# Forward substitution of the delta rule's diagonal blocks: from VectorE to GpSimd

## The chip, the cores and the metric

The kernel runs on one core of one Trainium2 chip. Its engines work side by side, each from an instruction queue of its own: TensorE (PE in the profile, PEld for its weight loads), VectorE (DVE), ScalarE (ACT), GpSimd (POOL) and the sync engine (SP), which here issues most of the transfers. They wait for one another by semaphores. The metric is device time in microseconds (us); less is better.

## The reference, cut to what matters

Two transformer blocks run one behind the other over 256 tokens of width 1024, all in float32. The first block has three mixers: a softmax attention with decay ("fox"), a stick-breaking attention, and a gated delta rule in chunks. The change lies in the delta rule, and what stands around it in the queues is the stick-breaking attention.

```python
def gated_delta_rule(q, k, v, g, beta):
    ...
    kk = jnp.einsum("nbhcd,nbhed->nbhce", kc, kc)
    a_mat = jnp.where(strict, bc[..., :, None] * kk * decay, 0.0) + jnp.eye(CHUNK, dtype=f32)
    ...
    sol = lax.linalg.triangular_solve(a_mat, rhs, left_side=True, lower=True)

def stick_breaking_attention(q, k, v):
    ...
        log_keep = jnp.where(mask, -jax.nn.softplus(z), 0.0)
        ...
        a = jnp.exp(jnp.where(mask, z + rc, -jnp.inf)).astype(vh.dtype)
```

The kernel inverts the unit lower triangular matrix of each head and each of two tiles of 128 tokens: first its 16x16 diagonal blocks by forward substitution, then it joins blocks of 16 to 32, 64 and 128 by products on TensorE.

## The kernel before

**Weights.** All weight matrices are cut into blocks of 128x2048 float32, numbered in order of use: gdn 0 to 5, sbqk 6 to 9, sbv 10 and 11, foxqk 12 to 15, foxv 16 and 17, gate_c 18 to 21, out_c 22 and on. A block is loaded in two halves by the sync queue into RAW, which has room for two blocks. So that TensorE can multiply in fp32r, ScalarE makes HI, the rounded block (L1480), and VectorE LO, the rest RAW - HI (L2019). Each has room for four blocks. `split_ahead(phase, Turn(j))` makes HI or LO of the block that stands four behind block j of the phase; on ScalarE it waits until TensorE is through with block j. The load of block n into RAW waits for LO of block n - 2, half by half. TensorE makes three products for each weight tile (L826, L827, L828): HI with XH, HI with XL, LO with XH.

**The substitution.** VectorE writes the delta rule's matrix into DL (delta_L, L2171) from the keys' products `kk0` and `kk1`. The sync queue takes its 64 diagonal blocks of 16x16 to HBM in eight transfers (L621) and back as DIAG_L (L623), one block to a partition: 64 partitions, 16x16 numbers. VectorE waits for diag_loaded and solves in 15 steps of two instructions each (L2189, L2190), every one linked to the one before by a semaphore; step j works on (j+1) x (15-j) numbers in each partition, which makes 680 over the 15 steps. The last sets diag_solved.

**What is queued around it.** On VectorE: LO of block 15; the absolute value of Z for the stick-breaking attention (L2180); the substitution; `split_ahead("foxqk", Turn(0))`, that is LO of block 16; the keep chain L2196 to L2198, which makes SP_ and needs ScalarE's Ln (keep_ln); LO of 17; LO of 18; then stick_arg, the subtraction of TensorE's sums from Z, for heads 0 and 1; LO of 19; stick_arg for heads 2 and 3; the heads' norm (heads_norm 1, which needs ScalarE's squares, then a root on GpSimd, then L2079) and LO of 20.

On the sync queue, after DIAG_L: a wait for diag_solved; the store of DIAG_T to HBM (L625); the load of block 18; a wait for the store; eight transfers into the diagonal of MP (L635); the loads of block 19 and on.

On ScalarE: HI of 16; Exp and Ln of SP_ (L1620, L1621); half of foxqk's result; HI of 17; HI of 18; the other half of foxqk's result; HI of 19; two squares for the heads' norm (L1630); HI of 20; the Exp of Z (L1635, stick_ready); foxv's result; HI of 21; a wait for diag_stored.

On TensorE: the blocks of foxqk 0 to 2; a wait for keep_ready; the sums rest_sums (L1078 to L1081) for heads 0 and 1; foxqk 3; those for heads 2 and 3; foxv; a wait for stick_ready; the products with the values (L1099, L1100); gate_c 0 (block 18); a wait for diag_placed and the turns T16 of MP (L983); gate_c 1 (block 19); the turns of the fox heads out of X (L983), then gate_c 2 (block 20).

On GpSimd: long before, the masks and the zeroing of MP and DIAG_T; two LO blocks (ON_POOL_CONV); `heads_root(0)`; a wait for the keys' products being taken; `heads_root(1)` (L710, L703, L704); then the products of DL with the level masks into MA (L789).

Of the kernel before, what the change touches and what calls it, by code (L numbers as in the profile page):

```python
# [193 lines left out]
N_DIAG = NT * HEADS * (P // 16)  # L194


def build(nc, A, out):
    f32, f32r = mybir.dt.float32, mybir.dt.float32r
    ALU = mybir.AluOpType
# [22 lines left out]
    with ctx:  # L222
# [37 lines left out]
        def at(name, kib, shape, dt=f32):  # L260
            size = 4
            for s in shape[1:]:
                size *= s
            assert kib * 1024 + size <= ARENA, name
            return nc.alloc_sbuf_tensor_at(name, shape, dt, offset=base + int(kib * 1024))
# [10 lines left out]
        DIAG_L, DIAG_T, DIAG_TERM = (at(f"diag_{n}", 40 + i, [N_DIAG, 16, 16]) for i, n in enumerate(["L", "T", "term"]))  # L276
# [87 lines left out]
        def sems(names):  # L364
            return [sem(n) for n in names.split()]
# [30 lines left out]
        diag_zeroed, diag_written, diag_loaded, diag_solved, diag_stored, diag_placed = sems(  # L396
            "diag_zeroed diag_written diag_loaded diag_solved diag_stored diag_placed")
# [38 lines left out]
        def small(name):  # L436
            return SMP[:, SMALL_ORDER[name] % 4, :]
# [11 lines left out]
        def small_is_taken(eng, name):  # L449
            eng.wait_ge(small_taken[SMALL_ORDER[name] % 4], SMALL_ORDER[name] // 4 + 1)  # L450
# [39 lines left out]
        def col(name, i=0):  # L490
            tile, row = COL_AT[name]
            return COL[tile][:, row + i:row + i + 1]
# [33 lines left out]
        def every(mask, n):  # L526

            return mask.unsqueeze(1).broadcast_to([P, n, mask.shape[1]])

        def by_head(ap, d=P):  # L530
            return ap.rearrange("p (h d) -> p h d", d=d)
# [140 lines left out]
        def _(pool):  # L672
            steps = [0]

            def link(ins):
                steps[0] += 1
                ins.then_inc(pool_step, 1)
                pool.wait_ge(pool_step, steps[0])
# [21 lines left out]
            def inverse_root(name, mean_square):  # L700

                n = ROOTS[name]
                link(pool.tensor_scalar(mean_square, mean_square, EPS, None, ALU.add))  # L703
                pool.tensor_tensor(ROOT[name], mean_square, MINUS_HALF[:, 0:n], ALU.pow).then_inc(root_ready, 1)  # L704

            def heads_root(n, mult):

                pool.wait_ge(heads_sums, NT * (n + 1))
                if mult != 1.0:
                    link(pool.tensor_scalar(HSS[n], HSS[n], mult, None, ALU.mult))  # L710
                inverse_root(f"heads{n}", HSS[n])
# [67 lines left out]

            for t in range(NT):  # L780
                small_is_taken(pool, f"kk{t}")
            heads_root(1, 1.0 / DH)


# [1222 lines left out]
        def _(dve):  # L2007
            steps = [0]

            def link(ins):  # L2010

                steps[0] += 1
                ins.then_inc(dve_step, 1)
                dve.wait_ge(dve_step, steps[0])
# [11 lines left out]
            def split_ahead(phase, t, halves=range(2)):  # L2026

                n = FIRST[phase] + t.j + RING
                if n < N_BLOCKS and n not in ON_POOL:
                    for half in halves:  # L2030
                        lo_half(n, half, t.count(lambda j: 2 * (FIRST[phase] + j + RING) + half + 1))
# [78 lines left out]
            for j in range(6):  # L2110
                dve.wait_ge(conv_base, 2 * j + 2)
                for i in range(2):
                    tile = 2 * j + i
                    u = acc("gdn", Turn(j))[:, i * 256:(i + 1) * 256]
                    for back in (1, 2, 3):
                        y = CONVF[:, tile, back:SEQ]
                        ins = dve.scalar_tensor_tensor(out=y, in0=u[:, 0:SEQ - back], scalar=col("gdn_conv", (3 - back) * 12 + tile),
                                                       in1=y, op0=ALU.mult, op1=ALU.add)
# [49 lines left out]
            for t in range(NT):  # L2168
                small_is_done(dve, f"kk{t}")
                for h in range(HEADS):  # L2170
                    ins = dve.scalar_tensor_tensor(out=DL[:, t, h, :], in0=small(f"kk{t}")[:, h * P:(h + 1) * P],  # L2171
                                                   scalar=BETA[:, t, h:h + 1], in1=MA[:, t, h, :], op0=ALU.mult, op1=ALU.mult)
# [6 lines left out]
                small_is_taken(dve, f"z{h}")  # L2179
            dve.scalar_tensor_tensor(out=SP_[:, :, :], in0=Z[:, :, :], scalar=-1.0, in1=Z[:, :, :], op0=ALU.mult, op1=ALU.max).then_inc(keep_abs, 1)  # L2180

            dve.wait_ge(diag_loaded, 16)
            dve.wait_ge(diag_zeroed, 3)
            for j in range(15):
                n, m = j + 1, 15 - j
                below = DIAG_L[:, n:16, j:n].rearrange("b r o -> b o r").broadcast_to([N_DIAG, n, m])
                solved = DIAG_T[:, 0:n, j:n].broadcast_to([N_DIAG, n, m])
                rest = DIAG_T[:, 0:n, n:16]
                link(dve.tensor_tensor(DIAG_TERM[:, 0:n, 0:m], below, solved, ALU.mult))  # L2189
                ins = dve.tensor_tensor(rest, rest, DIAG_TERM[:, 0:n, 0:m], ALU.subtract)  # L2190
                if j < 14:
                    link(ins)
            ins.then_inc(diag_solved, 1)
            split_ahead("foxqk", Turn(0))
            dve.wait_ge(keep_ln, 1)
            link(dve.scalar_tensor_tensor(out=SP_[:, :, :], in0=Z[:, :, :], scalar=0.0, in1=SP_[:, :, :], op0=ALU.max, op1=ALU.add))  # L2196
# [371 lines left out]
            for g in range(4):  # L2568
# [4 lines left out]
                for i in range(2):  # L2573
                    d = 2 * g + i
                    ins = dve.scalar_tensor_tensor(out=by_head(G[:, d, :]), in0=by_head(small(name)[:, i * SEQ:(i + 1) * SEQ]),
                                                   scalar=col("sgu_norm_g_2", d), in1=every(BS[:, g, :], NT),
                                                   op0=ALU.mult, op1=ALU.add)
# [42 lines left out]
            for c in range(2):  # L2620
                cols = slice(c * 512, (c + 1) * 512)
                a, b = Turn(2 * c), Turn(2 * c + 1)
# [82 lines left out]
```

## Time and profile before

| | us |
|---|---|
| median of 3 runs | 1179.21 (1178.56 to 1179.53) |
| profiled execution, its own time | 1175.5 |
| its span, first to last instruction | 1173.5 |
| TensorE busy | 1145.9 (98%) |
| VectorE busy | 744.9 (63%) |
| ScalarE busy | 589.5 (50%) |
| GpSimd busy | 97.6 (8%) |

The durations in the rows below come from the one profiled execution, whose mean granted TensorE clock was 0.997 of full speed. In a timeline row stand the start, the duration, the engine, the line, the operation, output and inputs, and in brackets how long the engine was idle before and what it waited for.

### The profile page before, as it was taken

How to read it: one execution, taken by the hardware profiler on the slowest of the kernel's cores; microseconds unless marked ns; L12 is line 12 of the kernel's file. 1: busy time of each engine (PE TensorE's matmuls, PEld its weight loads, DVE VectorE, ACT ScalarE, POOL GpSimd, SP SyncE). 2: the span in 40 equal slices, each digit the busy share in tenths (PEclk: the TensorE clock that was granted, in tenths of full speed). 3: DMA queues.
4: the chain of work that ended last, by engine and by line, in shares of the span. 5: the costliest groups of instructions: out<-in, count | busy, mean ns of one | idle time of the engine just before them, and what ended most of it. 6: DMA issues, size and time to landing. Idle time of an engine off the chain costs nothing.

```text
span 1173.5 us, 16543 instructions
## 1 busy us (share of the span) xinstructions
PE 1145.9 (98%) x6464; PEld 1003.2 (85%) x6464; DVE 744.9 (63%) x922; ACT 589.5 (50%) x781; POOL 97.6 (8%) x156
## 2 busy tenths in 40 slices
PE   7999999998999999999999999999989999999997
PEld 7998888897887999988888898799878878889885
DVE  5767767657666788764565454565775576554455
ACT  5675544444455666543454444454464355444352
POOL 5310211001010000000000000200500010000021
PEclk9999999999999999999999999999999999999999
DMA  8734564455553675556475556475465567555642
GB/s 237 219 119 140 162 201 139 129 176 186 177 187 119 216 224 175 191 193 202 135 242 184 177 177 215 143 227 158 138 222 193 176 191 249 180 178 179 207 135 71
DMA packets 124060, 210.33 MB, mean 179 GB/s; under 512 B 10980, under 2 KB 60249, under 8 KB 123993
## 3 DMA queue, kind: packets, MB, share of 16 engines
q1 hardware_dynamic: 120393, 199.17, 53.4%
q10 hardware_dynamic: 3504, 10.22, 2.5%
q8 instruction: 47, 0.77, 0.3%
q0 software_dynamic: 96, 0.01, 0.1%
q14 instruction: 20, 0.16, 0.0%
HBM read 208.19 MB, written 1.18 MB: 178 GB/s over the span
## 4 chain that ended last, share of the span: by engine, by line
PE 87%; DVE 6%; ACT 3%; issue 1%; DMA 1%; POOL 1%; SPq 0%; POOLq 0%; DVEq 0%; ACTq 0%
PE ACCP L826 26%; PE ACCP L828 26%; PE ACCP L827 26%; PE SMP L983 3%; DVE LO L2019 3%; PE SMP L976 2%; ACT HI L1480 1%; PE SMP L826 1%; PE SMP L828 1%; PE SMP L827 1%; DMA PRE_GAIN<-in_norm_mix_dram 1%; POOL STAT L704 0%; DMA diag_L<-scratch_diag_l 0%; POOL STAT L703 0%; DVE U L2582 0%
## 5 line engine op out<-in xcount | busy, mean ns | idle before, releaser
L2019 DVE TENSOR_TENSOR LO<-RAW,HI 128x1024 fp32r<-128x1024 f32 x367 | 439.1, 1235 | 242.5 <-ACT HI L1480 235.1
L1480 ACT ACTIVATE HI<-RAW 128x1024 fp32r<-128x1024 f32 x366 | 369.6, 1054 | 275.2 <-PE ACCP L828 240.9
L826 PE MATMUL ACCP<-HI,XH 128*128 128x512 f32 x688 | 271.1, 394 | 2.1 <-ACT SV L1488 1.6
L828 PE MATMUL ACCP<-HI,XL 128*128 128x512 f32 x688 | 268.1, 390 | 0.0
L827 PE MATMUL ACCP<-LO,XH 128*128 128x512 f32 x688 | 267.8, 389 | 0.0
L826 PE MATMUL ACCP<-XH,HI 128*128 128x256 f32 x688 | 196.6, 286 | 1.9 <-DVE XL L2064 1.9
L827 PE MATMUL ACCP<-XL,HI 128*128 128x256 f32 x688 | 195.4, 284 | 0.0
L828 PE MATMUL ACCP<-XH,LO 128*128 128x256 f32 x688 | 195.4, 284 | 0.0
L826 PEld LDWEIGHTS ACCP<-HI,XH 128*128 128x128 f32 x688 | 129.2, 188 | 28.5 <-issue 1.7
L828 PEld LDWEIGHTS ACCP<-HI,XL 128*128 128x128 f32 x688 | 129.1, 188 | 27.3
L827 PEld LDWEIGHTS ACCP<-LO,XH 128*128 128x128 f32 x688 | 129.3, 188 | 25.8
L826 PEld LDWEIGHTS ACCP<-XH,HI 128*128 128x128 f32 x688 | 132.9, 193 | 2.4 <-DVE LO L2019 2.2
L827 PEld LDWEIGHTS ACCP<-XL,HI 128*128 128x128 f32 x688 | 132.9, 193 | 0.1
L828 PEld LDWEIGHTS ACCP<-XH,LO 128*128 128x128 f32 x688 | 132.8, 193 | 0.0
L826 PE MATMUL ACCP<-HI,HH 128*128 128x512 f32 x328 | 128.1, 390 | 0.0
L828 PE MATMUL ACCP<-HI,HL 128*128 128x512 f32 x328 | 127.7, 389 | 0.0
L827 PE MATMUL ACCP<-LO,HH 128*128 128x512 f32 x328 | 127.6, 389 | 0.0
L703 POOL TENSOR_SCALAR STAT<-STAT 128x1 f32<-128x1 f32 (+3 forms) x30 | 11.6, 385 | 804.3 <-ACT XS L1736 453.1
L828 PEld LDWEIGHTS ACCP<-HI,HL 128*128 128x128 f32 x328 | 61.6, 188 | 12.7
L827 PEld LDWEIGHTS ACCP<-LO,HH 128*128 128x128 f32 x328 | 61.6, 188 | 12.6
L826 PEld LDWEIGHTS ACCP<-HI,HH 128*128 128x128 f32 x328 | 61.6, 188 | 12.6
L1488 ACT ACTIVATE XH<-SMP 128x512 fp32r<-128x512 f32 x36 | 20.5, 596 | 39.8 <-PE SMP L983 39.5
(379 smaller groups left out, 1146.4 us busy)
## 6 DMA issues: line engine op xcount, KB each, us to landing
RAW<-in_w_in_dram SPq DMA_DIRECT2D x104, 512.0 KB, 4.5
RAW<-in_w_up_dram SPq DMA_DIRECT2D x44, 512.0 KB, 4.6
RAW<-in_ffn_w_gate_dram SPq DMA_DIRECT2D x44, 512.0 KB, 4.5
RAW<-in_ffn_w_up_dram SPq DMA_DIRECT2D x44, 512.0 KB, 4.4
RAW<-in_ffn_w_down_dram SPq DMA_DIRECT2D x44, 512.0 KB, 4.3
RAW<-in_w_down_dram SPq DMA_DIRECT2D x22, 512.0 KB, 4.2
RAW<-in_w_out_dram SPq DMA_DIRECT2D x8, 512.0 KB, 4.0
RAW<-in_w_mkv_dram SPq DMA_DIRECT2D x8, 512.0 KB, 3.8
```

What stands on the lines that cost most here:

```text
L703: link(pool.tensor_scalar(mean_square, mean_square, EPS, None, ALU.add))
L826: pe.matmul(dst, lhs[0], rhs[0], start=start, stop=False)
L827: pe.matmul(dst, lhs[0], rhs[1], start=False, stop=False)
L828: return pe.matmul(dst, lhs[1], rhs[0], start=False, stop=stop)
L976: last = pe.matmul(small(name)[:, h * P:(h + 1) * P], lhs, rhs, start=True, stop=True)
L983: last = pe.transpose(small(name)[:, h * P:(h + 1) * P], source(h), IDENT[:, :])
L1480: act.activation(HI[:, n % RING, half_of(half)], RAW[:, n % RAWS, half, :], ACT.Copy).then_inc(hi_ready, 1)
L1488: act.activation(dst, src, ACT.Copy, scale=scale).then_inc(signal, 1)
L2019: dve.tensor_tensor(LO[:, s, c], RAW[:, n % RAWS, half, :], HI[:, s, c].bitcast(f32), ALU.subtract).then_inc(lo_ready[s], 1)
```

## The change

The 30 instructions of the substitution move from VectorE's program to GpSimd's, with their two waits (diag_loaded, diag_zeroed) and with the signal diag_solved. On GpSimd they stand between the wait for the keys' products and `heads_root(1)`. On VectorE `split_ahead("foxqk", Turn(0))` follows L2180 directly. Both engines have a helper `link` that does the same with a semaphore of their own. Operands, shapes and all transfers stay as they are.

```diff
             for t in range(NT):
                 small_is_taken(pool, f"kk{t}")
+            pool.wait_ge(diag_loaded, 16)
+            pool.wait_ge(diag_zeroed, 3)
+            for j in range(15):
+                n, m = j + 1, 15 - j
+                below = DIAG_L[:, n:16, j:n].rearrange("b r o -> b o r").broadcast_to([N_DIAG, n, m])
+                solved = DIAG_T[:, 0:n, j:n].broadcast_to([N_DIAG, n, m])
+                rest = DIAG_T[:, 0:n, n:16]
+                link(pool.tensor_tensor(DIAG_TERM[:, 0:n, 0:m], below, solved, ALU.mult))
+                ins = pool.tensor_tensor(rest, rest, DIAG_TERM[:, 0:n, 0:m], ALU.subtract)
+                if j < 14:
+                    link(ins)
+            ins.then_inc(diag_solved, 1)
             heads_root(1, 1.0 / DH)
...
             dve.scalar_tensor_tensor(out=SP_[:, :, :], in0=Z[:, :, :], scalar=-1.0, in1=Z[:, :, :], op0=ALU.mult, op1=ALU.max).then_inc(keep_abs, 1)
 
-            dve.wait_ge(diag_loaded, 16)
-            dve.wait_ge(diag_zeroed, 3)
-            for j in range(15):
-                n, m = j + 1, 15 - j
-                below = DIAG_L[:, n:16, j:n].rearrange("b r o -> b o r").broadcast_to([N_DIAG, n, m])
-                solved = DIAG_T[:, 0:n, j:n].broadcast_to([N_DIAG, n, m])
-                rest = DIAG_T[:, 0:n, n:16]
-                link(dve.tensor_tensor(DIAG_TERM[:, 0:n, 0:m], below, solved, ALU.mult))
-                ins = dve.tensor_tensor(rest, rest, DIAG_TERM[:, 0:n, 0:m], ALU.subtract)
-                if j < 14:
-                    link(ins)
-            ins.then_inc(diag_solved, 1)
             split_ahead("foxqk", Turn(0))
```

## Rows read from the trace of the kernel before

**Rows 1.** Page, part 1: busy us, share of the span, instructions.

```profile
PE 1145.9 (98%) x6464; PEld 1003.2 (85%) x6464; DVE 744.9 (63%) x922; ACT 589.5 (50%) x781; POOL 97.6 (8%) x156
```

**Rows 2.** TensorE's waits (us, times, longest), and busy us between 120.7 and 172.

```profile
PE SMP L1078 <- DVE SP__72 L2198: 0.7, 1, 0.7
...
core 0: us, PE busy (x) PEld busy (x) DVE busy (x) ACT busy (x) POOL busy (x), PEclk, DMA share, GB/s
120.70:172.00 51.30, 51.30 (x269) 44.08 (x269) 35.47 (x34) 26.66 (x33) 10.49 (x7) 1.00 0.59 187
```

**Rows 3.** Timeline of VectorE around and behind the substitution.

```profile
107.88 0.17 DVE L2189 TENSOR_TENSOR diag_term<-diag_L,diag_T 64x15 f32<-64x15 f32 x1 [3.23 <-DMA diag_L<-scratch_diag_l]
...
115.15 2.34 DVE L2019 TENSOR_TENSOR LO<-RAW,HI 128x1024 fp32r<-128x1024 f32 x2
117.42 1.74 DVE L2196 SCALAR_TENSOR_TENSOR SP__72<-Z,SP__72 128x1536 f32<-128x1536 f32 x1
...
119.92 0.69 DVE L2198 TENSOR_TENSOR SP__72<-SP__72,BEFORE 128x512 f32<-128x512 f32 x1
...
140.04 4.53 DVE L2079 TENSOR_TENSOR X<-X,STAT 128x1024 f32<-128x1024 f32 x2 [3.87 <-POOL STAT L704]
```

**Rows 4.** Timeline of ScalarE from HI of 16 to the Exp of Z.

```profile
109.14 2.01 ACT L1480 ACTIVATE HI<-RAW 128x1024 fp32r<-128x1024 f32 x2 [5.42 <-PE ACCP L828]
...
113.84 1.49 ACT L1621 ACTIVATE SP__72<-SP__72 128x1536 f32<-128x1536 f32 x1
...
120.22 1.06 ACT L1480 ACTIVATE HI<-RAW 128x1024 fp32r<-128x1024 f32 x1 [2.02 <-DMA RAW<-in_w_in_dram]
122.13 1.06 ACT L1480 ACTIVATE HI<-RAW 128x1024 fp32r<-128x1024 f32 x1 [0.85 <-DMA RAW<-in_w_in_dram]
...
131.43 2.00 ACT L1630 ACTIVATE XS<-X 128x1024 f32<-128x1024 f32 x2
136.11 2.01 ACT L1480 ACTIVATE HI<-RAW 128x1024 fp32r<-128x1024 f32 x2 [2.68 <-PE ACCP L828]
...
139.43 1.49 ACT L1635 ACTIVATE Z<-Z 128x1536 f32<-128x1536 f32 x1
```

**Rows 5.** Timeline of the sync queue; last row: KB and us to landing.

```profile
115.25 0.47 SPq L625 DMA_DIRECT2D scratch_diag_t<-diag_T  x1
116.38 0.37 SPq L551 DMA_DIRECT2D RAW<-in_w_in_dram  x1
...
117.52 0.37 SPq L551 DMA_DIRECT2D RAW<-in_w_in_dram  x1
117.99 3.72 SPq L635 DMA_DIRECT2D delta_P<-scratch_diag_t  x8
...
scratch_diag_t<-diag_T SPq DMA_DIRECT2D x1, 64.0 KB, 1.9
```

**Rows 6.** Timeline of TensorE, three starts.

```profile
120.66 0.44 PE L1078 MATMUL SMP<-BIG_NOT_BEFORE_R,IDENT_R 128*128 128x384 f32 x1 [0.68 <-DVE SP__72 L2198]
...
141.35 0.59 PE L1099 MATMUL SMP<-Z,SV 128*128 128x256 f32 x2
...
155.77 1.91 PE L983 MATMUL SMP<-IDENT,X 128*128 128x128 f32 x16
```

**Rows 7.** Timeline of GpSimd: large and small instructions elsewhere in the kernel.

```profile
829.60 1.04 POOL L807 TENSOR_TENSOR S2A<-C 128x510 f32<-128x510 f32 x1
...
836.13 2.73 POOL L807 TENSOR_TENSOR S<-S2B 128x1524 f32<-128x1524 f32 x1
...
1164.57 0.58 POOL L816 TENSOR_TENSOR STAT<-STAT 128x1 f32<-128x1 f32 x1 [19.74 <-DVE STAT L2661]
1165.23 0.22 POOL L703 TENSOR_SCALAR STAT<-STAT 128x1 f32<-128x1 f32 x1
```

**Rows 8.** GpSimd and VectorE side by side: timelines, and VectorE's mean from 164.2 to 168.8.

```profile
950.04 1.12 POOL L703 TENSOR_SCALAR STAT<-STAT 128x1 f32<-128x1 f32 x1 [6.22 <-ACT XS L1736]
...
949.86 1.22 DVE L2019 TENSOR_TENSOR LO<-RAW,HI 128x1024 fp32r<-128x1024 f32 x1
...
L2019 DVE TENSOR_TENSOR LO<-RAW,HI 128x1024 fp32r<-128x1024 f32 x2 | 4.4, 2260 | 1.4 <-ACT HI L1480 1.4
...
164.13 3.52 POOL L789 TENSOR_TENSOR delta_A<-delta_L,LEVEL 128x512 f32<-128x512 f32 x2 [20.65 <-PE SMP L976]
```

## The prediction

> **What bounds the kernel now.** The page of the profile is read first: TensorE is busy 1145.9 of 1173.5 us and GpSimd 97.6 [rows 1]. So a microsecond leaves the time only where TensorE itself stands still. The waits by engine come next: of TensorE's few waits one lies beside the change, the 0.7 us in front of L1078 for VectorE's L2198 [rows 2]. The table by stretches shows the engine without a gap from 120.70 to 172.00 [rows 2]. The timelines of the five queues between 100 and 142 us then tell what everyone does around the substitution.
>
> VectorE waits 3.23 us for DIAG_L, starts the substitution at 107.88 and is through at 115.15. Then come LO of block 16 (split_ahead("foxqk", 0)) and the keep chain L2196 to L2198 [rows 3]; LO of blocks 17 and 18 follows. The chain ends at 120.61, TensorE starts L1078 at 120.66 [rows 3, 6].
>
> The sync queue hangs on the same event. Behind its wait on diag_solved stand, in this order: the store of DIAG_T (115.25), both halves of block 18 (116.38, 117.52), the eight transfers into MP from 117.99, and block 19 and all later weights [rows 5]. ScalarE works in order too: HI of 18, HI of 19, two squares up to 133.43, HI of 20 at 136.11, a table load, the Exp of Z from 139.43 to 140.92 [rows 4]. TensorE takes that Exp at 141.35 (L1099) [rows 6]. HI of 20 starts as TensorE finishes a foxv block. ScalarE has about 2.7 us of idle time in front of it, from 133.43 to 136.11, and 0.4 us behind the Exp. That is all the slack between the weights and TensorE here.
>
> **What leaves VectorE.** 30 instructions in 115.15 - 107.88 = 7.3 us, and the 3.2 us of waiting. LO of 16 can then follow HI of 16, ready in halves at about 110.2 and 111.15, and ends near 112.6. The keep chain waits for the Ln, which ends at 113.84 + 1.49 = 115.33 [rows 4]; its three instructions span 120.61 - 117.42 = 3.2 us [rows 3], so it ends at 118.5. TensorE reaches L1078 at 120.66 - 0.68 = 119.98, so the wait goes and 0.7 us is won, with 1.4 us to spare for disturbance by GpSimd. Nothing else on TensorE waits for VectorE up to 142: 0.7 us is the whole direct gain. LO of 17 follows up to about 121.
>
> **What GpSimd gets.** It is idle here in the trace of before: its next work is the root for which VectorE waits 3.87 us up to 140.04 [rows 3], so its queue itself delays nobody unless the end comes after 136. It starts when DIAG_L lands, 107.9. No row shows a small two-input product in short rows on it. From below: the adds of 510 and 1524 elements took 1.04 and 2.73 us [rows 7]. That is 1.69 / 1014 = 1.67 ns an element and 1.04 - 510 x 0.00167 = 0.19 us fixed. The mean instruction here has (sum of (j+1)(15-j) over 15 steps)/15 = 680/15 = 45 elements, 0.08 us; every step is linked, and a linked pair shows 0.08 us between its end at 1165.15 and the next start at 1165.23 [rows 7]. Sum 0.35 us, 30 of them 10.4 us. From above: an add of one element took 0.58 us [rows 7]; 0.58 + 0.08 + 0.08 = 0.74, times 30 = 22 us. I take 0.45, nearer to the lower end, since the large adds bear a small fixed part and the one-element add ran beside a VectorE instruction; with 0.1 us more for rows of 1 to 15 elements read at a stride of 64 bytes (estimate): 13.5 us.
>
> The Trainium skill (GPSIMD Engine Reference, Performance pitfalls for Q7 kernels) says that reads with a step over 8 bytes take about half again as long per element. No row of before shows it; on the 15 products alone it would add 680 x 0.83 ns = 0.6 us, an estimate from that page and the row's slope, and it is no term of the sum.
>
> **What the two engines do to each other.** A one-element GpSimd instruction that began at 950.04, just behind the start of a VectorE LO at 949.86 (ending 951.08), took 1.12 us and ended at 951.16; the same form took 0.22 elsewhere [rows 8, 7]. And two LO on VectorE beside GpSimd's masks took 2.26 us each [rows 8], where two in a row take 2.34 together [rows 3]. So they serialise where both read two operands. The Trainium skill (SBUF, Who interferes with whom) says that the later one blocks fully; the first pair agrees. By that rule alone, without any turn for GpSimd between VectorE's instructions, the sum below would be about 2 us later.
>
> Then, at 0.45 us each: 5 GpSimd instructions before LO of 16 starts (107.95 to 110.2); about one behind each of its two halves, 2; 6 between 112.6 and 115.4; one behind each of the three chain and two LO instructions, 5. That is 18 by 121.5. VectorE has then nothing to do, as block 18 is not there; the remaining 12 take 5.4 us. End E = 127, against 115.2 before.
>
> **What is late next.** From the end E, with durations of before. The store issues at once and lands 1.9 us later [rows 5]; block 18 issues at E + 0.5 and E + 0.95; the MP transfers start at E + 2.0 and take 3.72 (+0.06) us of the queue [rows 5]; block 19 issues at E + 5.8 and E + 6.25. A half's HI started 120.22 - 116.38 = 3.84 us behind its issue, the second 4.6 [rows 4, 5]. So HI of 18 ends at E + 6.6, LO of 18 at E + 7.9; block 20 issues at E + 6.75 and E + 7.95. HI of 19 ends at E + 6.25 + 4.6 + 1.06 = E + 11.9. Squares 2.0 and HI of 20, 2.0: E + 15.9 (its weights are there by E + 12.6). Table load 1.28, Exp 1.49 [rows 4]: E + 18.7. TensorE starts L1099 there, against 141.35. The change is E + 18.7 - 141.35 = E - 122.6, never under -0.7. At E = 127: +4.4 us. The 0.7 us is in it already.
>
> The other moved pieces cost nothing. MP is placed by E + 9.2 (the last of eight transfers issues at E + 5.3, and even the 3.84 us of a weight half would do), TensorE takes it behind L1099; ScalarE's wait on diag_stored stands behind the Exp as well. The squares end at E + 13.9 = 140.9 and not at 133.4, so the root on GpSimd, VectorE's scaled heads (L2079, ending at 144.6 before) and LO of 20 come 7.5 us later, 3 more than TensorE; TensorE turns those heads at 155.77 [rows 3, 6], 11 us behind them, which covers it. What GpSimd's move could cost there if the cover were gone is those 3 us. TensorE has no gap up to 172 in which the loss could be won back.
>
> **Rivals.** (1) GpSimd is quick enough: the result is the same time. At the lower price and without blocking E = 107.9 + 10.4 = 118.3: -0.7 us, 1178.5. At the lower price with blocking about 20 instructions are through by 121.5 and E = 125, +2.4. Even at 0.45 without blocking E = 121.4, -0.7. For it: nothing in the rows is as small as these steps, and the lower price comes from two sizes of plain rows. Against it: rows 8. The break-even is E = 121.9 for the whole gain, E = 122.6 for none. (2) GpSimd is much slower: at 0.74 with blocking 3 + 2 + 4 + 5 = 14 through by 121.5, the rest 11.8 us, E = 133, +10.7 us, 1190. For it: the one small two-input row; against: a VectorE instruction ran beside that one. (3) Faster by over 0.2%: VectorE's 10.5 us free would have to save 2.4 us of TensorE, which waits 0.7. Only if the earlier LO blocks pull later stages; the rows give no place, so about 1178.5 at best. (4) The blocking falls on VectorE: each chain instruction waits for one small GpSimd instruction, 3 x 0.45 = 1.35 us, which the 1.4 us of spare covers; nothing gained then but nothing lost, inside rival 1's band.
>
> **How the numbers follow.** The profiled execution took 1175.5 us for a span of 1173.5; that is 3.7 below the median of 1179.21, to which I add the difference. Forecast: 1179.2 + 4.4 = 1183.6. About 0.2% (2.4 us) is what a measurement of this kernel can tell from no change, which is E = 125. Chances: forecast case, E from 125 to 131, 0.46; rival 1 with rival 4, 0.32; rival 2, E beyond 131, 0.17; rival 3, 0.05. So slower 0.63, same 0.32, faster 0.05. The range runs from the full gain, 1178.3, to rival 2's 1190.5; the forecast case alone spans 1181.6 to 1187.6.
>
> **What would show it.** In the profile after: the 0.7 us in front of L1078 gone (step 1). The GpSimd products and differences from 107.9 at 0.35 to 0.55 us apart where VectorE is idle, and stretched to the end of VectorE's instruction where it is not (step 2). The store of DIAG_T on the sync queue at E, block 18 right behind it, HI of 18 and 19 waiting for the transfer (step 3). A new TensorE wait in front of L1099 for the Exp of Z, E + 18.7 - 140.7 long (step 4). I am wrong if E is under 122, if the wait appears elsewhere (L1078, the T16 turns, a foxv or gate_c block's LO), or if small GpSimd instructions cost over 0.8 us.

## The result: slower by about half a per cent, with TensorE waiting behind the sync queue

The changed kernel took 1183.46 us (median of 5 runs, 1179.41 to 1187.32) against 1178.56 us (1174.87 to 1179.53) for the kernel before. The ratio is 1.0049, with a 95% interval of 1.0028 to 1.0070. Run again beside the other experiments it gave 1184.81 us and 1.0061 (1.0045 to 1.0078). The forecast was 1183.6 us.

The profiled execution of the changed kernel is the slowest of its runs (1187.32 us, span 1185.4), that of before one of the fastest of its kernel (1175.5 us). The two spans, 11.9 us apart, must therefore not be read as the effect. Of these 11.9 us, 7.0 had come by the turns of MP (156.47 against 149.43) and 4.9 came behind them. 3.2 of those lie far from the change, between 750 and 920 us: there the granted clock of TensorE is 0.66 in the 10 us from 875.

The page of the changed kernel, part 1, against [rows 1]:

```profile
PE 1151.7 (97%) x6464; PEld 1007.1 (85%) x6464; DVE 738.9 (62%) x892; ACT 589.2 (50%) x781; POOL 112.1 (9%) x186
```

VectorE lost 30 instructions and GpSimd has 30 more. TensorE's waits between 100 and 170 us, against [rows 2] (us in total, times, longest), beside one of 1.6 us for SV that the kernel before has as well; the changed source has L1111 for the products that were L1099:

```profile
PE SMP L1111 <- ACT Z L1647: 5.7, 1, 5.7
```

The 0.7 us in front of the keep chain's sums are gone, and 5.7 us in front of the stick-breaking products have come. The timelines of GpSimd, VectorE, the sync queue, ScalarE and TensorE in the same execution, one fence for each, show the way there, against [rows 3 to 6]:

```profile
108.89 0.21 POOL L789 TENSOR_TENSOR diag_term<-diag_L,diag_T 64x15 f32<-64x15 f32 x1 [30.74 <-DMA diag_L<-scratch_diag_l]
...
109.48 1.28 POOL L789 TENSOR_TENSOR diag_term<-diag_L,diag_T 64x28 f32<-64x28 f32 x1
110.84 1.10 POOL L790 TENSOR_TENSOR diag_T<-diag_T,diag_term 64x28 f32<-64x28 f32 x1
...
114.56 1.91 POOL L790 TENSOR_TENSOR diag_T<-diag_T,diag_term 64x60 f32<-64x60 f32 x1
116.55 0.69 POOL L789 TENSOR_TENSOR diag_term<-diag_L,diag_T 64x63 f32<-64x63 f32 x1
...
125.32 0.24 POOL L790 TENSOR_TENSOR diag_T<-diag_T,diag_term 64x15 f32<-64x15 f32 x1
```

```profile
114.56 1.76 DVE L2196 SCALAR_TENSOR_TENSOR SP__72<-Z,SP__72 128x1536 f32<-128x1536 f32 x1 [2.72 <-ACT SP__72 L1633]
...
117.71 2.60 DVE L2031 TENSOR_TENSOR LO<-RAW,HI 128x1024 fp32r<-128x1024 f32 x2
```

```profile
125.59 0.46 SPq L625 DMA_DIRECT2D scratch_diag_t<-diag_T  x1
126.09 1.12 SPq L551 DMA_DIRECT2D RAW<-in_w_in_dram  x2
127.54 4.77 SPq L635 DMA_DIRECT2D delta_P<-scratch_diag_t  x8
132.35 8.10 SPq L551 DMA_DIRECT2D RAW<-in_w_in_dram  x6
```

```profile
130.19 1.06 ACT L1492 ACTIVATE HI<-RAW 128x1024 fp32r<-128x1024 f32 x1 [12.79 <-DMA RAW<-in_w_in_dram]
...
137.74 1.06 ACT L1492 ACTIVATE HI<-RAW 128x1024 fp32r<-128x1024 f32 x1 [0.43 <-DMA RAW<-in_w_in_dram]
138.70 1.99 ACT L1642 ACTIVATE XS<-X 128x1024 f32<-128x1024 f32 x2
140.59 1.99 ACT L1492 ACTIVATE HI<-RAW 128x1024 fp32r<-128x1024 f32 x2
142.60 1.28 ACT L1647 ACT_TABLE_LOAD   x1
143.90 1.48 ACT L1647 ACTIVATE Z<-Z 128x1536 f32<-128x1536 f32 x1
```

```profile
98.22 0.59 PE L1077 MATMUL SMP<-SQK 128*128 128x256 f32 x2
...
145.43 1.22 PE L1111 MATMUL SMP<-Z,SV 128*128 128x256 f32 x2 [5.70 <-ACT Z L1647]
...
156.47 1.03 PE L995 MATMUL SMP<-IDENT,delta_P 128*128 128x128 f32 x8
```

The reader is to see three things. GpSimd's instructions take 0.21 to 0.32 us or, when VectorE reads two operands in the same moment, up to 1.91. Everything on the sync queue starts at 125.59, right behind GpSimd's last instruction, and not at 115.25. ScalarE has been idle for 12.79 us when the first half of block 18 lands, and from then on it waits only for the second half of 18 (0.39 us) and the two halves of block 19 (2.58 and 0.43): it has no idle time left in front of HI of 20, where it had 2.68 us before [rows 4].

A fourth thing was not in the forecast. These are the stretches of the same execution around the wait (busy us by engine and number of instructions, then TensorE's granted clock, DMA share and GB/s):

```profile
140.00:144.00 4.00, 0.00 (x0) 0.00 (x0) 3.24 (x5) 3.97 (x5) 0.55 (x2) 1.00 0.88 288
144.00:152.00 8.00, 6.57 (x21) 5.59 (x22) 4.99 (x3) 5.43 (x7) 6.39 (x3) 0.57 0.00 2
152.00:160.00 8.00, 8.00 (x41) 6.70 (x40) 5.51 (x7) 1.16 (x2) 0.00 (x0) 1.00 0.93 325
```

TensorE stood still from 139.7 to 145.4. Its clock was still at 1.00 up to 144, and from 145 to 151 at the lower of its two levels, 1.2 GHz. It made 21 products in 6.6 us there and 41 in the next 8. From the start of the stick-breaking products to the turns of MP it took 156.47 - 145.43 = 11.0 us, against 149.43 - 141.35 = 8.1 before: 3.0 us that the wait alone does not explain. The two rows of before for this and for the next section:

```profile
99.03 0.59 PE L1065 MATMUL SMP<-SQK 128*128 128x256 f32 x2
...
149.43 1.03 PE L983 MATMUL SMP<-IDENT,delta_P 128*128 128x128 f32 x8
```

### The profile page after: what moved, and what is told of

The parts are those of the page before. It is cut to its first block, busy times and chain, and to the rows that moved or that the text cites. A ratio compares the mean times of both kernels' runs of the same rounds, so it can differ in the third digit from the quotient of the medians.

```text
span 1185.4 us, 16543 instructions
## 1 busy us (share of the span) xinstructions
PE 1151.7 (97%) x6464; PEld 1007.1 (85%) x6464; DVE 738.9 (62%) x892; ACT 589.2 (50%) x781; POOL 112.1 (9%) x186
## 4 chain that ended last, share of the span: by engine, by line
PE 82%; DVE 6%; ACT 3%; DMA 3%; issue 2%; POOL 2%; SPq 1%; POOLq 0%; DVEq 0%; ACTq 0%
PE ACCP L838 24%; PE ACCP L840 24%; PE ACCP L839 24%; PE SMP L995 3%; DVE LO L2031 3%; PE SMP L988 2%; ACT HI L1492 2%; DMA RAW<-in_w_in_dram 1%; PE SMP L838 1%; PE SMP L839 1%; PE SMP L840 1%; POOL diag_T L790 1%; DVE XS L2067 1%; DMA X<-in_x_dram 1%; POOL diag_term L789 1%
## 5 line engine op out<-in xcount | busy, mean ns | idle before, releaser
L703 POOL TENSOR_SCALAR STAT<-STAT 128x1 f32<-128x1 f32 (+3 forms) x30 | 11.9, 396 | 810.0 <-ACT XS L1748 455.9
```

## The experiments

The executions start up to 1.5 us apart, so their times are compared from one fixed point, the start of TensorE's stick-breaking scores (99.03 in the trace of before, 98.22 in the first of the changed kernel). In the table, E is the moment when the store of DIAG_T is issued, "Exp wait" TensorE's wait in front of the stick-breaking products, "stretch" the time from the fixed point to the turns of MP (149.43 - 99.03 = 50.4 us before), and "clock loss" how much longer than 8.1 us the piece from the stick-breaking products to those turns took. The last column is the timed ratio to before with its 95% interval; each kernel was timed 5 to 12 times, beside before.

| kernel | E | Exp wait | stretch - 50.4 | clock loss | ratio |
|---|---|---|---|---|---|
| before | 16.2 | 0 | 0 | 0 | 1 |
| changed, first | 27.4 | 5.7 | +7.9 | 3.0 | 1.0049 (1.0028 to 1.0070) |
| after_again | 25.5 | 3.0 | +2.3 | 0.1 | 1.0061 (1.0045 to 1.0078) |
| loads_first | 27.1 | 0 | -1.0 | 0 | 0.9984 (0.9973 to 0.9996) |
| loads_first_2 | 27.2 | 0 | -1.0 | 0 | 0.9983 (0.9971 to 0.9995) |
| late_signal | 28.3 | 2.2 | +7.7 | 1.8 | 1.0049 (1.0031 to 1.0067) |
| late_signal_7 | 23.7 | 0 | +0.6 | 0.1 | 1.0004 (0.9992 to 1.0015) |
| filled_wait | 26.2 | 0 | +4.3 | 0 | 1.0040 (1.0025 to 1.0055) |
| products_twice | 32.3 | 10.9 | +11.9 | 1.8 | 1.0083 (1.0066 to 1.0100) |
| placed_later | 27.4 | 3.3 | +4.3 | 1.8 | 1.0013 (1.0000 to 1.0027) |
| loads_first_vector | 26.7 | 0 | +0.1 | 0 | 1.0000 (0.9987 to 1.0013) |
| substitution_alone | 21.6 | 0 | +6.8 | 0 | 1.0035 (1.0020 to 1.0050) |

In loads_first_vector the substitution ends as early as before; the store stands behind the loads there. In substitution_alone the clock falls in front of the piece that the column measures, and so does the first of two falls in late_signal. Each row has one profile beside its timed runs, and E moves between executions. A profile's stretch and the timed ratio agree in sign, but they lie up to 5 us apart: after_again has +2.3 against 7.2 us timed, placed_later +4.3 against 1.5, substitution_alone +6.8 against 4.1. Behind the turns of MP the profiles differ as well: from there to the end of the span before took 1024.1 us, the others 1024.8 to 1028.9.

**after_again**: no edit.

> The changed kernel once more, beside the others on one chip. In its first profile GpSimd ended the substitution at 125.56 us, TensorE waited 5.7 us in front of the stick-breaking products, and the granted TensorE clock was 0.50 to 0.68 in the 6 us behind the wait. Theory A (the blocked sync queue makes block 18 and 19 late, and that the Exp of Z): the wait is there again, 5 to 6.5 us long, and the kernel is 5 to 8 us slower than before (wait 5.7, clock about 3, gain about 1). Theory B (the loss came from elsewhere in that one execution, and the wait is chance): the wait's length differs by more than 2 us or is absent, and the time is within 2 us of before.

The same wait is there, in the same place:

```profile
PE SMP L1111 <- ACT Z L1647: 3.0, 1, 3.0
```

It is 3.0 and not 5 to 6.5 us long. That is 2.7 shorter than at first, more than the 2 us that the expectation gave to theory B (chance). The parts of the difference are in the trace: E came 1.9 us earlier (DIAG_L took 4.5 us to land, 6.2 in the first), and the eight transfers took 3.73 us of the queue and not 4.77. The clock stayed at 1.00. The time, 1.0061 or 7.2 us, is what theory A said and not within B's 2 us. The wait is a property of the kernel, its length is one of the execution.

**loads_first** and **loads_first_2**: the same kernel, on the changed one.

```diff
             sp.dma_start(DIAG_L[:, :, :]...).then_inc(diag_loaded, 16)
+            for j in range(3):
+                load("gate_c", Turn(j), t_block(w["w_in"], C_GATE + DM * 2 + 512 * (j // 2), j % 2))
             sp.wait_ge(diag_solved, 1)
...
                 for j in range(4):
-                    load(f"gate_{g}", Turn(j), ...)
+                    if g != "c" or j == 3:
+                        load(f"gate_{g}", Turn(j), ...)
```

> The changed kernel, with the sync queue issuing the loads of blocks 18, 19 and 20 ahead of its wait for the solved blocks; substitution on GpSimd as in the change. Theory A (the queue behind the wait is what costs): the end of the substitution stays near 125.5, the wait in front of the stick-breaking products goes from 5.7 to under 0.5 us, the clock stays full there, and the time is about 0.9 us under before (the wait at the keep chain, which is gone too), so within 1.5 us of it. Theory B (GpSimd's reads slow VectorE's LO blocks and keep chain, and that makes TensorE wait): the wait stays at 3 us or more and the time at 4 us or more over before.

> loads_first once more, to see whether its 0.9984 (0.9973 to 0.9996) holds. Theory A: the wait at the keep chain is gone whenever DIAG_L lands late as well, so 0.9 us in a quiet execution and more on average: ratio 0.9975 to 0.9995, no wait for the Exp of Z. Rival: it was chance, ratio 0.9995 to 1.001.

The sync queue of this kernel (first timing):

```profile
112.34 12.45 SPq L551 DMA_DIRECT2D RAW<-in_w_in_dram  x6
126.94 0.47 SPq L627 DMA_DIRECT2D scratch_diag_t<-diag_T  x1
```

The solved blocks come as late as in the changed kernel (27.1 behind the fixed point), but six halves are on their way by then, and both waits of TensorE, the old and the new one, are gone. The time is 1.9 us under before, and 2.0 in the second timing; 0.9, and no more than 1.5, had been expected. Theory B falls: GpSimd worked beside VectorE here no shorter (108.70 to 126.92, 18.2 us), and cost TensorE nothing.

**late_signal** and **late_signal_7**: on the kernel before; nine linked fills and a last one, or six and a last one.

```diff
+            pool.wait_ge(diag_solved, 1)
+            for _ in range(9):
+                link(pool.memset(PAUSE[:, :], 0.0))
+            pool.memset(PAUSE[:, :], 0.0).then_inc(diag_late, 1)
...
-            sp.wait_ge(diag_solved, 1)
+            sp.wait_ge(diag_late, 1)
```

> The kernel before, substitution on VectorE; but the sync queue waits for a signal that GpSimd gives only after ten linked fills of 128x1024 numbers behind the substitution (about 10.4 us, one of which takes 0.96 us), so at about 125.6. Nothing but the signal is late: VectorE's work and its time stay as before, and the fills read nothing. Theory A: the same wait in front of the stick-breaking products as in the change, 5 to 6.5 us, and the clock falls behind it; 7 to 10 us slower than before (the 0.9 us at the keep chain are not won). Theory B (it is GpSimd's arithmetic beside VectorE): within 1.5 us of before.

> late_signal with seven fills instead of ten: the solved blocks are signalled 7.2 to 7.3 us behind the substitution on VectorE, at 122.4 to 122.9 in the time of the trace of before. Theory A puts the break-even of the signal at 122.6: the wait for the Exp of Z is 0 to 1.5 us (10 fills: 2.2 and 2.6 more of waiting in front of the keep chain), the clock stays at 1.00 behind it, and the time is within 2 us of before. Rival (there is no slack, and every microsecond of a late signal counts from the start): 5 us or more over before.

TensorE's waits with ten fills (a third one, 1.6 us for SV, is in every kernel):

```profile
PE SMP L1084 <- DVE SP__72 L2204: 2.6, 1, 2.6
PE SMP L1105 <- ACT Z L1641: 2.2, 1, 2.2
```

With ten fills the time is 5.8 us over before, though VectorE did the substitution: a late signal alone makes a loss of that size. It is less than the 7 to 10 expected, and the wait for the Exp is 2.2 us and not 5 to 6.5. In the profile the waiting is split: 2.6 us in front of the keep chain, because DIAG_L took 6.4 us to land in this execution, and 2.2 in front of the stick-breaking products. The clock fell behind both (0.57 from 122 to 126, 0.66 from 145 to 150). With seven fills E is 23.7, where the prediction's break-even of 122.6 - 99.03 = 23.6 lies, and there is no wait for the Exp and no difference in time beyond the interval. So the slack is as the prediction computed it, and behind it the cost begins.

**filled_wait**: on the changed kernel.

```diff
+            small_bank_free(pe, "so0")
+            for _ in range(30):
+                pe.matmul(small("so0")[:, 0:384], IDENT_R[:, :], BIG_NOT_BEFORE_R[:, :], start=True, stop=True)
             pe.wait_ge(stick_ready, 1)
```

> The changed kernel, with 30 more products of 384 columns on TensorE in front of its wait for the Exp of Z (about 0.18 us each, 5.3 us), into a bank that is overwritten behind them: extra work whose results nobody uses. Theory A2 (the idle time of TensorE brings the clock down, and the clock costs 3 us on top of the wait): the clock stays at 1.00 behind the wait, the stick-breaking products and block 18 run at their pace of before, and the time is about 3 us under the changed kernel. Theory C (the clock falls there whatever TensorE does, or its fall is chance): clock 0.5 to 0.7 behind the wait again, time equal to the changed kernel within 1 us.

```profile
140.00:152.00 12.00, 12.00 (x65) 11.01 (x65) 8.22 (x6) 8.13 (x10) 6.98 (x5) 1.00 0.41 140
```

The clock stayed at 1.00, although the products with the values started 0.65 us later than the Exp allowed (144.86 against 144.21). The time is 2.8 us under the changed kernel by the medians (1182.03 and 1184.81), but the intervals overlap, and one of the two profiles of the changed kernel kept its clock as well. Every fall of the clock in the table comes during a wait of TensorE or behind one, but not every wait brings one, and the length does not decide it: the clock stayed up after 3.0 us in after_again and fell after 2.6 and 2.2 us in late_signal. So what the clock adds to the timed loss of the changed kernel is not shown.

**products_twice**: on the changed kernel.

```diff
-                link(pool.tensor_tensor(DIAG_TERM[:, 0:n, 0:m], below, solved, ALU.mult))
+                for _ in range(2):
+                    link(pool.tensor_tensor(DIAG_TERM[:, 0:n, 0:m], below, solved, ALU.mult))
```

> The changed kernel with each of the 15 products of the substitution done twice on GpSimd (extra work, same result), so about 15 x 0.36 = 5.4 us more behind the same signal. Theory A (each microsecond of the substitution beyond about 122 is one of TensorE's): the end moves from 124.4 to 125.6 to 130 to 131, the wait in front of the stick-breaking products is 8 to 11 us, the clock falls behind it, and the time is 5 to 7 us over the changed kernel. Theory E (the wait is set by something that comes after the substitution and has slack of its own, such as TensorE's block or ScalarE's order): the time grows by less than 3 us.

The signal came 4.9 and 6.8 us later than in the two profiles of the changed kernel and the wait was 10.9 us, 5.2 and 7.9 longer. So in the profile it is about one for one, as theory A says. The timed runs do not settle it: 1.0083 is 9.8 us over before, which is 2.6 to 4.0 more than the changed kernel, with overlapping intervals, and theory E's bound of 3 lies inside that. By the medians it is 11.2 us over before, 5.0 to 6.3 more than the changed kernel, as theory A has it.

**placed_later**: on the changed kernel.

```diff
-                    if g == "c" and j == 0:
+                    if g == "c" and j == 2:
                         sp.wait_ge(diag_stored, 16)
```

> The changed kernel with the eight transfers into MP issued behind the loads of blocks 19 and 20 and not ahead of them; the store and block 18 still wait for the solved blocks. Theory A with the terms of the prediction: block 19 issues about 4.4 us earlier, the Exp of Z ends at the end of the substitution + 16.4 (set by block 20, whose room comes free with LO of 18) and not + 19, the wait goes from 3 to 5.7 us to 0 to 1.3 us, the clock stays full, and the time is 0 to 2 us over before. Rival (block 18 alone is what counts, the eight transfers do not): the wait stays at 3 us or more.

1.0013 is 1.5 us over before: in the timed runs some three quarters of the loss are gone with the eight small transfers out of block 19's way. In the profile the Exp ended 17.4 us behind E, not 16.4, the wait was still 3.3 us, which is what the rival said, and the clock fell behind it. But E lay at 27.4 here, where the changed kernel's first profile had 5.7. Both the wait for the solved blocks and the eight transfers count; the runs don't split them to the microsecond.

**loads_first_vector**: loads_first's edit on the kernel before.

> The kernel before, substitution on VectorE, with the sync queue issuing the loads of blocks 18, 19 and 20 ahead of its wait for the solved blocks. Theory A (in the kernel before the queue's order costs nothing, since its wait ends early enough, and the move of the substitution itself wins what loads_first showed): time within 1 us of before, the wait at the keep chain still 0.7 us or more. Theory D (loads_first was faster by 1.9 us because of the earlier loads and not because of VectorE): this is as fast as loads_first, 1.5 us or more under before.

```profile
PE SMP L1081 <- DVE SP__72 L2201: 0.8, 1, 0.8
```

Nothing changed: 1.0000, and the wait for the keep chain is still there. Theory D falls. So it takes both: the reordered queue alone wins nothing (block 18 has to wait for LO of block 16 there, and leaves at 115.75), the moved substitution alone loses, together they win 1.9 us.

**substitution_alone**: on the changed kernel.

```diff
+            dve.wait_ge(diag_solved, 1)
             split_ahead("foxqk", Turn(0))
```

> The changed kernel, but VectorE waits for the solved blocks ahead of LO of block 16, so that GpSimd works with nothing on VectorE beside it. Contention theory: the 30 instructions then take 0.30 to 0.41 us from start to start, 10.7 to 11.2 us in all (16.2 to 16.7 in the two profiles of the change), the end comes at about 119; TensorE waits 4 to 6 us for the keep chain in its place and little or nothing for the Exp of Z; the time is 3 to 8 us over before. Rival (GpSimd's long instructions are its own, from strided rows): seven or more of them stay above 0.6 us.

```profile
L789 POOL TENSOR_TENSOR diag_term<-diag_L,diag_T x15: 212/301/333, 110.7 to 120.9; 64x15 f32<-64x15 f32 x2, 64x28 f32<-64x28 f32 x2, 64x39 f32<-64x39 f32 x2, 64x48 f32<-64x48 f32 x2
L790 POOL TENSOR_TENSOR diag_T<-diag_T,diag_term x15: 213/278/317, 111.0 to 121.2; 64x15 f32<-64x15 f32 x2, 64x28 f32<-64x28 f32 x2, 64x39 f32<-64x39 f32 x2, 64x48 f32<-64x48 f32 x2
```

These are the two lines of the substitution (shortest, median and longest in ns, first and last start in us). The next is from TensorE's waits in the same kernel:

```profile
PE SMP L1090 <- DVE SP__72 L2199: 6.2, 1, 6.2
```

None of the 30 took over 0.34 us, the whole 121.41 - 110.68 = 10.7 us. The first profile of the changed kernel has 125.56 - 108.89 = 16.7, with seven instructions of 0.64 to 1.91 us, as many as VectorE has instructions with two operands in SBUF in that time, and with 8.0 us together where their forms take about 2.1 alone. So 5.9 of GpSimd's 16.7 us are VectorE's doing. The rival, strided rows, falls. The price is a wait of TensorE for the keep chain of 6.2 us, a little over the 4 to 6 expected; the time, 4.1 us over before, is in the expected band.

## Why the prediction was right, step by step

**The 0.7 us on VectorE.** Right: the wait at the keep chain is gone in both profiles, and the stretch to its sums is 0.8 us shorter. VectorE was hardly disturbed: LO of 16 and of 17 took 2.41 and 2.60 us, where LO of 16 took 2.34 before, and L2196 took 1.76 instead of 1.74. The term is a little small on average, since the old wait grows when DIAG_L lands late (2.6 us in late_signal); loads_first wins 1.9 us by the clock of the timed runs and 1.0 in its profiles. That the late landing is the whole of the difference is argued, not shown.

**E = 127.** It came at 125.56, or 126.4 counted from the fixed point of before. Three terms were off and partly cancelled. The price of an instruction was put at 0.45 us and is 0.358; the lower bound of 0.35, from the large adds [rows 7], was right. The one-element add of 0.58 in the same rows ended 0.05 us behind a two-operand instruction of VectorE (1164.41 to 1165.10), so it was most likely a blocked one. The 0.1 us added for strided rows is in no run: product and difference at 64x64 lie 0.02 us apart. The work of 13.5 us is thus 10.7. The blocking, by turns with VectorE from [rows 8], added 19.1 - 13.5 = 5.6 us in the prediction and 5.9 in the first profile: right. The start was put at 107.9; DIAG_L landed 6.2 us behind its issue there instead of 4.5, and the start came 1.0 later by the trace's own time, 1.8 counted from the fixed point. The nearest line of the prediction is its own aside, the lower price with blocking, which gave E = 125. Of the page that was named, SBUF in the Trainium skill (Who interferes with whom), the rule that the later one blocks fully agrees with the instruction of 1.91 us on GpSimd beside VectorE's L2196, which spans it to its end, and with the long instructions of [rows 8] (last section). The stride rule of the Trainium skill (GPSIMD Engine Reference, Performance pitfalls for Q7 kernels) is borne out at most in part: the product at 64x64 took 0.33 us and the difference, with short steps, 0.31, where the rule would put 0.05 between them (64 x 0.83 ns, an estimate from that page and the slope in [rows 7]).

**E + 18.7 to the Exp.** It was 19.8 in the first profile and 18.9 in the second. Of the 1.1 us missing in the first the eight transfers make 1.0, with 4.77 us on the queue instead of 3.72. In filled_wait, late_signal and products_twice it was 19.7 to 20.1 with transfers of 3.64 to 3.83 us: there a half of block 19 landed later than the sum has it. So the term is 0.2 to 1.4 us small. The chain itself, store, block 18, transfers, block 19, HI, squares, HI of 20, table, Exp, stands in the trace link by link, and late_signal_7 found its break-even within the reading. One sentence of the prediction does not fit its own sum: the 2.7 and 0.4 us of ScalarE are not all the slack. The break-even of 122.6 lies 7.4 us behind 115.2, since ScalarE also stood idle for 5.37 us ahead of foxqk's second half in the trace of before:

```profile
128.56 1.09 ACT L1488 ACTIVATE X<-ACCP 128x512 f32<-128x512 f32 x2 [5.37 <-PE ACCP L828]
```

**The sum.** +4.4 us was forecast for the median; the two timings give 5.8 and 7.2 us, from 1.0049 and 1.0061, with lower bounds of 3.3 and 5.3, so the second lies clear above the forecast. With the E of the two profiles (126.4 and 124.5 by before's time) the prediction's own formula gives 3.8 and 1.9 us; the stretches were 7.9 and 2.3 longer. The step that was missing is the clock: the prediction priced TensorE's wait at its length and not at what the wait does to the products behind it, which is 3.0 us in the first profile and 0.1 in the second. The way of the loss was foreseen; that 1183.6 and 1183.46 lie so close is luck. The term too large (price) and the terms too small or left out (the way to the Exp, the clock) have opposite signs, and before measured 0.6 us less beside the changed kernel than the 1179.2 from which the forecast starts.

**The rivals.** Rival 1 (quick enough) was right in its price and wrong where it left out the blocking: 108.9 + 10.7 = 119.6 would have been within the slack. Rival 2 did not come. Rival 3's "no place" for a win of 2.4 us holds. Rival 4 was seen in a mild form, 0.02 us on L2196 and 0.3 on LO of 17, and cost nothing.

## What to carry to other kernels

Before a piece of work moves to a slower engine, look who waits for its result in an in-order queue, and what stands behind that wait: here one semaphore held up weights that had nothing to do with it. Moving the loads ahead of the wait was free, and it turned a loss of half a per cent into a gain of 0.16%. And count what the engine it leaves will do meanwhile: GpSimd needed 10.7 us alone, and 16.7 beside VectorE's two-operand instructions.

## What the runs showed of the hardware

Small two-operand instructions on GpSimd in 64 partitions took 0.21 us for 15 elements and 0.33 for 64, with 0.08 us between linked ones. Beside VectorE they took up to 1.93 (loads_first), while VectorE's own were lengthened by up to 11%. Two long ones took turns: in [rows 8] GpSimd's masks took 1.29 and 2.28 us and the two LO on VectorE 2.22 and 2.30 instead of 1.2, each but the first ending 1.0 to 1.2 us behind the one before it on the other engine. So VectorE waits too where GpSimd began first; beside short instructions it has little to wait for.

TensorE's granted clock fell to 0.50, the 1.2 GHz level, with waits of 5.7 and 10.9 us, during them already (in the latter 1.00 from 140 to 144 and 0.50 from 146 to 152), and in substitution_alone with one of 6.2 us (0.52 from 125 to 130). After a wait of 3.0 us it stayed at 1.00 in one profile, after 3.3 us it fell in another (0.76 from 145 to 150), and in late_signal after 2.6 and 2.2 us. The same is seen far from the change: a wait of 3.0 us for ScalarE near 870 is in both kernels, and the clock stayed at 1.00 behind it before and fell to 0.50 (875 to 880) in the first profile of the changed kernel. One small transfer, DIAG_L of 64 KB, took between 4.3 and 6.4 us to land behind two weight halves, from one execution to the next.
